# Layer-norm sums, added squares, the PLE gate's tanh and LN1's first residual sum in PSUM banks, and the first mean one contraction tile later

## The reference, cut to what matters

```python
x = layer_norm(DEEPNORM_ALPHA * x + merged @ w_out[i], ln1_g[i], ln1_b[i])       # "LN1"
ffn = jnp.square(jax.nn.relu(x @ w_ff_in[i])) @ w_ff_out[i]
ple = jax.nn.sigmoid(x @ w_ple_gate[i]) * (p[i] @ w_ple[i])
x = layer_norm(DEEPNORM_ALPHA * x + ffn + ple, ln2_g[i], ln2_b[i])               # "LN2"

def layer_norm(x, g, b):
    mu = mean(x); var = mean(square(x - mu))
    return (x - mu) * rsqrt(var + 1e-5) * g + b
```

## Time and profile before

| | |
|---|---|
| time, median of 3 runs | 2654.56 us (2651.69, 2654.56, 2655.14) |
| span of the profiled execution | 2653.1 us |
| the profiled execution's own time | not given apart from its span; the span is 1.5 us under the median |
| PE, PEld busy | 97%, 75% |
| DVE, ACT, POOL busy | 59%, 43%, 40% |
| mean granted TensorE clock | 0.990 of full speed |

### The profile page before, as it was taken

One profiled execution on the slowest core, in us unless ns is written; L12 is line 12 of the kernel. 1 busy time (PEld: TensorE's weight loads), 2 busy tenths in 40 slices (PEclk: granted clock), 3 DMA queues, 4 the chain that ended last, 5 costly groups with the idle time before them and its releaser, 6 DMA issues.

```text
span 2653.1 us, 35398 instructions
## 1 busy us (share of the span) xinstructions
PE 2565.0 (97%) x12424; PEld 1983.9 (75%) x12424; DVE 1565.4 (59%) x2510; ACT 1147.6 (43%) x1984; POOL 1062.1 (40%) x440
## 2 busy tenths in 40 slices
PE   8999999999999899999999999998999999999998
PEld 6867667788888688676677888885887776887776
DVE  6147748843322751676588234227689766689765
ACT  3345444433322433544535233325247554347554
POOL 4432213354444344222233454442447512447512
PEclk9999999999999999999999999998999999999999
DMA  5321112233233243111122223231334211234211
GB/s 201 100 80 56 48 48 87 72 103 97 93 96 102 71 124 100 64 61 49 48 96 88 95 95 98 93 109 49 95 96 147 80 33 53 91 101 148 75 38 56
DMA packets 66891, 227.94 MB, mean 86 GB/s; under 512 B 8784, under 2 KB 8912, under 8 KB 66768
## 3 DMA queue, kind: packets, MB, share of 16 engines
q1 hardware_dynamic: 66192, 224.73, 26.2%
q10 hardware_dynamic: 576, 1.57, 0.2%
HBM read 216.57 MB, written 2.10 MB: 82 GB/s over the span
## 4 chain that ended last, share of the span: by engine, by line
PE 74%; DVE 12%; DVEq 9%; ACT 2%; issue 2%; POOL 0%; ACTq 0%; DMA 0%; SPq 0%
PE bank L404 20%; PE bank L406 19%; PE bank L405 19%; DVEq L2337 5%; PE bank L592 3%; PE bank L619 3%; PE bank L605 2%; PE bank L595 1%; PE bank L873 1%; DVEq L2359 1%; PE bank L1253 1%; PE bank L847 1%; DVE ffn_sum L1796 1%; PE bank L1225 1%; PE bank L1224 1%
## 5 line engine op out<-in xcount | busy, mean ns | idle before, releaser
L500 POOL TENSOR_TENSOR w_lo<-w_raw,w_hi 128x1024 fp32r<-128x1024 f32 x404 | 1017.8, 2527 | 1575.6 <-ACT w_hi L413 1569.7
L404 PE MATMUL bank<-x_hi,w_hi 128*128 128x512 f32 x2048 | 828.8, 405 | 28.3 <-DVE x_lo L2567 10.6
L406 PE MATMUL bank<-x_hi,w_lo 128*128 128x512 f32 x2048 | 804.9, 393 | 0.0
L405 PE MATMUL bank<-x_lo,w_hi 128*128 128x512 f32 x2048 | 803.5, 392 | 0.0
L413 ACT ACTIVATE w_hi<-w_raw 128x1024 fp32r<-128x1024 f32 x400 | 419.5, 1055 | 439.7 <-PE bank L406 355.3
L404 PEld LDWEIGHTS bank<-x_hi,w_hi 128*128 128x128 f32 x2048 | 388.4, 190 | 128.4 <-issue 29.7
L406 PEld LDWEIGHTS bank<-x_hi,w_lo 128*128 128x128 f32 x2048 | 387.8, 189 | 83.6
L405 PEld LDWEIGHTS bank<-x_lo,w_hi 128*128 128x128 f32 x2048 | 388.6, 190 | 75.0 <-issue 1.2
L404 PE MATMUL bank<-rhs_hi,w_hi 128*128 128x512 f32 x624 | 245.2, 393 | 3.3 <-DVE rhs_lo L1698 3.3
L405 PE MATMUL bank<-rhs_lo,w_hi 128*128 128x512 f32 x624 | 243.7, 390 | 0.0
L406 PE MATMUL bank<-rhs_hi,w_lo 128*128 128x512 f32 x624 | 243.4, 390 | 0.0
(11 more groups left out here) (410 smaller groups left out, 3248.0 us busy)
## 6 DMA issues: line engine op xcount, KB each, us to landing
w_raw<-w SPq DMA_DIRECT2D x404, 512.0 KB, 3.4
work<-proj SPq DMA_DIRECT2D x60, 64.0 KB, 2.0
ln_in<-x SPq DMA_DIRECT2D x4, 512.0 KB, 7.2
out<-residual SPq DMA_DIRECT2D x8, 256.0 KB, 2.1
p_raw<-p ACTq DMA_DIRECT2D x2, 512.0 KB, 3.5
silu_z_nsa<-b_q SPq DMA_DIRECT2D x16, 64.0 KB, 2.3
work<-b_q SPq DMA_DIRECT2D x16, 64.0 KB, 2.3
silu_z_nsa<-b_kc SPq DMA_DIRECT2D x8, 64.0 KB, 2.0
```

The costliest lines, as they stand in the source:

```text
L404: nc.tensor.matmul(out, wh, xh, start=first, stop=False)
L405: nc.tensor.matmul(out, wh, xl, start=False, stop=False)
L406: S.last = nc.tensor.matmul(out, wl, xh, start=False, stop=last)
L500: S.nc.gpsimd.tensor_tensor(S.wl[s][:, :], S.raw[s][:, :], S.wh[s][:, :].bitcast(F32), ALU.subtract).then_inc(S.lo_ready[s], 1)
```

## The change

Sums that were held in SBUF are held in PSUM banks while they grow. In `ln_sums_dve` tile 0 is copied to `X[2]`, tiles 1 and 2 are added there, and the last addition goes to `wk[0]`, which the matmul reads; the rest sum starts with a copy of tile 4 to `X[2]` (a step at x = 4 that was not there) and ends in `ln_rest_sum`. ACT writes the first square of a norm to `X[1]`, the sum of squares grows there, and only its last addition goes to `wk[0]`. The PLE gate's tanh is written back to the unit's own bank, DVE's first step with it too, and the bank is handed back to PE by DVE, after its second step, and no longer by ACT; `tanh_used` goes and `tanh_done` comes. In LN1, for x up to 4, the low part of the residual is added first, in the bank, and the bank is handed back one step later. In `shifted` the step between goes to `X[3]`. The first mean is taken one contraction tile (three matmuls) later in unit 4.

```diff
@@ pe_unit
-        if middle and k == KT // 2:
+        if middle and k == KT // 2 + 1:
@@ square_buffer, add_square
-    return S.wk[j % 4 if j < 4 else 1 + (j - 4) % 3]
+    return (S.X[1], *S.wk[1:4])[j] if j < 4 else S.wk[1 + (j - 4) % 3]
...
-    S.nc.vector.tensor_tensor(S.wk[0][:, :], S.wk[0][:, :], square_buffer(S, j)[:, :], ALU.add).then_inc(S.sq_added, 1)
+    out = S.wk[0] if j == (6 if n < 2 * DEPTH else 5) else S.X[1]
+    S.nc.vector.tensor_tensor(out[:, :], S.X[1][:, :], square_buffer(S, j)[:, :], ALU.add).then_inc(S.sq_added, 1)
@@ ln_sums_dve
-    add = lambda out, a, b: S.nc.vector.tensor_tensor(out, a, b, ALU.add)
-    s, off = S.wk[0][:, :], S.lnoff[:, :]
-    if 1 <= x <= 3:
-        m = add(s, seq(t, 0) if x == 1 else s, seq(t, x))
-        if x == 3:
-            m.then_inc(S.ln_sum, 1)
-            for j in range(4):
-                ln_less_first_dve(S, dve, n0, t, j)
+    s = S.X[2][:, :]
+    if x == 0:
+        S.nc.vector.tensor_copy(s, seq(t, x))
+    if x in (1, 2):
+        S.nc.vector.tensor_tensor(s, s, seq(t, x), ALU.add)
+    if x == 3:
+        S.nc.vector.tensor_tensor(S.wk[0][:, :], s, seq(t, x), ALU.add).then_inc(S.ln_sum, 1)
+        for j in range(4):
+            ln_less_first_dve(S, dve, n0, t, j)
     if x == 4:
         ln_less_first_dve(S, dve, n0, t, x)
-    if x in (5, 6):
-        m = add(off, seq(t, 4) if x == 5 else off, seq(t, x))
-        if x == 6:
-            m.then_inc(S.ln_rest, 1)
+        dve.drain()
+        S.nc.vector.tensor_copy(s, seq(t, x))
+    if x == 5:
+        S.nc.vector.tensor_tensor(s, s, seq(t, x), ALU.add)
+    if x == 6:
+        S.nc.vector.tensor_tensor(S.lnoff[:, :], s, seq(t, x), ALU.add).then_inc(S.ln_rest, 1)
@@ a_scalar, the gate of LN2
-            act.wait_ge(S.tanh_used, L * KT + x + 1)
-            nc.scalar.activation(S.wk[4 + x % 2][:, :], S.ps[s][:, :], ACT.Tanh, scale=0.5).then_inc(S.bank_free[s], 1)
+            nc.scalar.activation(S.ps[s][:, :], S.ps[s][:, :], ACT.Tanh, scale=0.5).then_inc(S.tanh_done, 1)
@@ a_vector, LN1
-            h = S.wk[4 + x % 2][:, :]
+            h = S.X[3][:, :]
...
-            nc.vector.tensor_tensor(h, h, seq(S.xh, x).bitcast(F32), ALU.add)
+            nc.vector.tensor_tensor(S.wk[4 + x % 2][:, :], h, seq(S.xh, x).bitcast(F32), ALU.add)
...
-                nc.vector.scalar_tensor_tensor(out=t, in0=seq(S.xh, x).bitcast(F32), scalar=ALPHA,
-                                               in1=S.ps[s][:, :], op0=ALU.mult, op1=ALU.add).then_inc(S.bank_free[s], 1)
+                bank = S.ps[s][:, :]
+                nc.vector.scalar_tensor_tensor(out=bank, in0=seq(S.xl, x).bitcast(F32), scalar=ALPHA, in1=bank,
+                                               op0=ALU.mult, op1=ALU.add)
                 dve.drain()
-                nc.vector.scalar_tensor_tensor(out=t, in0=seq(S.xl, x).bitcast(F32), scalar=ALPHA,
-                                               in1=t, op0=ALU.mult, op1=ALU.add)
+                nc.vector.scalar_tensor_tensor(out=t, in0=seq(S.xh, x).bitcast(F32), scalar=ALPHA, in1=bank,
+                                               op0=ALU.mult, op1=ALU.add).then_inc(S.bank_free[s], 1)
@@ a_vector, LN2
-            dve.wait_ge(S.bank_free[s], G(u) + 2)
-            a, y = S.wk[6 + x % 2][:, :], seq(S.yacc, x)
-            nc.vector.scalar_tensor_tensor(out=a, in0=S.wk[4 + x % 2][:, :], scalar=1.0, in1=seq(S.plep, x),
-                                           op0=ALU.add, op1=ALU.mult).then_inc(S.tanh_used, 1)
+            dve.wait_ge(S.tanh_done, L * KT + x + 1)
+            a, y = S.ps[s][:, :], seq(S.yacc, x)
+            nc.vector.scalar_tensor_tensor(out=a, in0=a, scalar=1.0, in1=seq(S.plep, x), op0=ALU.add, op1=ALU.mult)
             dve.drain()
             m = nc.vector.scalar_tensor_tensor(out=y, in0=a, scalar=0.5, in1=y, op0=ALU.mult, op1=ALU.add)
+            m.then_inc(*((S.ln_d, 1) if x > 4 else (S.bank_free[s], 1)))
+            dve.drain()
             if x > 4:
-                m.then_inc(S.ln_d, 1)
-            dve.drain()
+                free_bank(S, dve, u)
```

More of the change, by code:

```diff
@@ L277, in plan @@
     S.p_ready = sem("p_ready")
-    S.tanh_used = sem("tanh_used")
+    S.tanh_done = sem("tanh_done")
     S.out_done = sem("out_done")
@@ L2554, in setup_vector @@
     nc = S.nc
-    prime(S, dve, [(b, 1) for b in S.bank_free] + [(S.stk_oev, 1), (S.first_added, 1), (S.mc_ready, 1), (S.merge_x, 2), (S.ffn_h, 2), (S.tanh_used, 2)])
+    prime(S, dve, [(b, 1) for b in S.bank_free] + [(S.stk_oev, 1), (S.first_added, 1), (S.mc_ready, 1), (S.merge_x, 2), (S.ffn_h, 2)])
     nc.vector.memset(S.ones[:, :], 1.0 / D)
```

## The result

The changed kernel takes 2633.98 us (median of 4 runs, 2630.82 to 2637.14), the kernel before 2654.85 (2651.69 to 2657.83). The ratio is 0.9919, 95% interval 0.9908 to 0.9931: some 21 us less, well beyond the 0.2% that can be told. The forecast was 2639.0, with a range of its own of 2636 to 2642 and a wider one, with two of the rivals, of 2633.5 to 2646. Over all executions on record the mean time is 2654.9 us before (83 whose clock is on record, without three of 3600 us and more) and 2634.7 after (9), 20.2 us apart, and the mean granted clock 0.9916 and 0.9927. The profiled execution has a span of 2631.5 us and a time of 2633.26.

The account below looks back on a forecast made before the run. PE, busy 97% of the span, bounds the kernel. LN1's 2 x 2.76 plus LN2's 4.3 and 5.8 take 15.6 us off 2653.1, making 2637.5; with 1.5 for the median, 2639.0, range 2636 to 2642 (2633.5 to 2646 with A and D).

Parts of the forecast that it names:

- What a bank operand is worth: DVE steps beside POOL's split: two SBUF operands stand until it is through (1.91 us), one bank operand doesn't (0.69).
- Part 1: First mean of each layer norm: PE's wait goes, 1.78 us in LN1, 2.40 in LN2.
- the 1.51 us of clock: LN2 of layer 1: low clock behind PE's idle stretch, counted as gained; bound 0 to 1.51 us.
- That is the price of the later mean, and it falls on DVE: LN1: the later mean makes DVE turn to unit 4 about 0.5 us late.
- Part 2: Tail of a norm: DVE in time for tile 7; LN1 gains 0.98 us more; LN2 totals 4.3 and 5.8.
- Part 3: Copies, bank steps and later bank returns cost nothing or little: DVE bank steps 0.70 us, at 0.754 1 us in all.
- The dearer bank access: Skill's rule of 0.065 us more per step moved to a bank; would make the sum 0.3 us smaller.
- A: Only the first mean gains, DVE stays the bound at the tail: gain 9.9 us, time 2644.7; chance 0.12.
- B: No change, PE waits a little further on for weights or POOL: 2651 to 2657 us; chance 0.06.
- C: Slower, writing a bank being read or following another engine in it is much slower: 2667 us; chance 0.03.
- D: More gain: LN1's tail gives DVE's 3.4 us, not PE's 2.76; clock falls less often; 19 us, 2635.5; chance 0.05.
- What follows a layer norm ... is moved as a whole: Root, eight tiles and `x_lo` behind each layer norm hang on the last four matmuls and move with them.

Follow-up runs that it names:

- before_light_split: Kernel before, with POOL subtracting only 8 of 1024 columns in the weight splits that fall in the layer norms' units: 2640.92 us, ratio 0.9949.
- all_but_mean_later: Changed kernel with the first mean put back where it was: 2633.89 us, ratio 0.9919 to the kernel before.
- padded_loop: Kernel before, with 15 memsets of 128x1 and a drain put ahead of the second model's convolution stage in DVE's program: 2650.33 us, ratio 0.9987.
- before_light_conv: Kernel before, with POOL subtracting only 8 of 1024 columns for units 16 to 19 of the second model's first layer: 2650.42 us, ratio 0.9981.

## Where the prediction was right, and the step that failed

**What a bank operand is worth: right, and shown.** A step with two SBUF operands stands beside POOL's split, one with a bank operand doesn't; before_light_split has the short steps without any bank. The Trainium skill, SBUF — State Buffer, section Who interferes with whom, states it: a DVE instruction with two SBUF inputs contends with a GpSimd one that reads SBUF, one with at most one SBUF input doesn't, outside the modes that use both ports. The rows agree, with 0.69 against 2.7 us.

**Part 1: right.** The waits ahead of line 980 went in all four norms, and the 1.51 us of clock with the last. The later mean isn't needed for it in LN1 (all_but_mean_later has no wait there either) and is worth 0.5 us in each LN2. "That is the price of the later mean, and it falls on DVE" held only because nothing in the tail could be stretched any more: alone, the same edit cost 5 us in each LN1.

**Part 2: right.** LN1 2.76 forecast, 2.9 and 3.0 measured; LN2 of layer 0 4.3 and 4.45; of layer 1 5.8 and 6.0. Sum 15.6 against 16.4. The 0.2 us more in LN1 are a cost that I didn't count: behind each wait the pair of matmuls that had waited keeps PE 0.10 us longer (from line 1005 to line 988 it is 0.96 us in the earlier trace rows, against the usual 0.86), and two waits went. DVE was in time for tile 7, with 0.78 us to spare in LN1 where I had 0.2.

**Part 3: right.** Steps into a bank took 0.69 to 0.70 us, ACT's in-place tanh 0.58. The dearer bank access that I weighed there doesn't show after either. Rivals A, B and C are out by the same rows. D was near in size, but not by its first mechanism: LN1's tail gave no more than PE's own. Its second, that the clock falls less often, stays open (see below).

**The step that failed: the sum stopped at the norms.** "What follows a layer norm ... is moved as a whole" holds for what hangs on it, but I took all the rest of the program to be moved as a whole too: it stands in the sum at nothing, without a reason. In the second model's first layer it wasn't moved as a whole. The same kind of collision as in the norms, a step of 2.89 us beside POOL's split where it takes 0.69 alone, stood in the trace of before, and the added DVE instructions ahead of it shortened the loop's gaps and so dissolved it: 2.3 us in both traces of the changed kernel, in padded_loop and in before_light_conv. With it and the norms' 16.4 the sum is 18.7, and the time 2636 us.

**What is left.** The two kernels' mean times lie 20.2 us apart, so some 1.5 us are left. They are of the size of the clock's share. As an estimate, (1 - mean granted clock) x span is the time lost to the low clock: 22.4 us before and 19.3 after, over the executions named with the result. Of the 3.1 us between them the last norm has 1.5, which the forecast counted; 1.6 are outside it, with a standard error of about 1.0. That the changed kernel has less of the low clock on the average would account for what is left, but these executions don't show it beyond their noise, and nothing here shows why it should. The medians' 20.9 us and the traces' 21.6 (3.4 of it clock outside the norms, against some 1.3 in the second trace) were in part luck.

## What to carry to other kernels

Before an engine's step is called slow, look at what POOL does in the same microseconds: here some 17 us of a 2650 us kernel hung on two-operand DVE steps beside a subtraction on POOL, and one operand in a bank, or a shorter step on POOL, cured it. Move the operands first and the waits second: with the operands where they were, POOL's work coming 0.7 us sooner cost 10 us in the two LN1. And when a change is to be summed up, look for the same collision in stages that it doesn't edit: their order against POOL can turn over by less than a microsecond.

## What was unexpected of the hardware

- The idle time between two passes of the same DVE loop was 0.66 us or 0.56 us, depending on what stood ahead of it in DVE's program; 15 memsets and a drain that compute nothing made the kernel 0.13% faster (interval 0.04 to 0.22%).
- A three-step group of added squares (2.25 us in the kernel before) took 4.28 us when it began 0.26 us ahead of POOL's subtraction. A single step that begins ahead of POOL's passes: 0.69 us when it began 0.36 us ahead, 2.82 when it began 0.13 us behind.
- With PE equally busy (18.62 and 18.63 of 20 us), the granted clock of the same stretch was 0.91 in one execution and 1.00 in another; each such stretch is worth about 1.6 us there.
